# Sixteen overlapped steps per head pair in the stick-breaking layer of a two-layer trunk

## What is computed

```python
logits = einsum('bhqd,bhsd->bhqs', qb, k) * scale        # strict: key before query
log_beta = log_sigmoid(logits)
log_keep = where(strict, log_beta - logits, 0.0)
between = cumsum(log_keep, reverse=True) - log_keep
weights = where(strict, exp(log_beta + between), 0.0)
y = weights @ v
```

## Time and profile before

| | |
|---|---|
| median of 3 runs | 1549.23 us (1548.76 to 1550.56) |
| the profiled execution | 1549.6 us, span 1547.8 us |
| granted TensorE clock, mean | 0.962 |
| prologue, up to the first score | 0 to about 95 us |
| stick layer's eight pairs | about 95 to 770 us |
| output projection, differential layer, its output projection | to 1547.8 us |

### The profile page before, as it was taken

The page is one execution under the profiler, slowest core; times in us unless marked ns, Lnnn a source line. Parts: engine busy times, 40 slices in busy tenths (PEclk is TensorE's granted clock), DMA queues, the critical chain, the costliest instruction groups (busy, mean ns, idle before and its releaser), DMA issues. The chain is left out here.

```text
span 1547.8 us, 23695 instructions
## 1 busy us (share of the span) xinstructions
PE 1394.5 (90%) x7206; PEld 1142.0 (74%) x7206; DVE 1049.6 (68%) x1812; ACT 875.4 (57%) x1710; POOL 558.8 (36%) x334
## 2 busy tenths in 40 slices
PE   6888989898999999986996899999999999995898
PEld 3577777777777777775875678887878878783776
DVE  4559888887969797978558656556565655557415
ACT  4536465555656464555345457667676767667322
POOL 2025546555656465636222412131121212122204
PEclk8889999999999999997998899999999999996999
DMA  9011121112021211121034011000100010002015
GB/s 347 25 54 56 42 62 46 54 50 58 27 74 35 68 41 54 57 98 63 1 123 136 28 38 31 27 27 27 41 27 27 27 41 27 27 14 109 1 52 180
DMA packets 112649, 89.82 MB, mean 58 GB/s; under 512 B 2553, under 2 KB 101090, under 8 KB 112610
## 3 DMA queue, kind: packets, MB, share of 16 engines
q1 hardware_dynamic: 112320, 89.15, 18.3%
q10 hardware_dynamic: 290, 0.18, 0.1%
HBM read 80.92 MB, written 8.40 MB: 58 GB/s over the span
## 5 line engine op out<-in xcount | busy, mean ns | idle before, releaser
L711 PE MATMUL bank<-h_hi,w_hi 128*128 128x512 f32 x976 | 396.8, 407 | 10.9 <-DVE h_lo L612 4.7
L711 PE MATMUL bank<-h_lo,w_hi 128*128 128x512 f32 x976 | 394.2, 404 | 0.0
L711 PE MATMUL bank<-h_hi,w_lo 128*128 128x512 f32 x976 | 391.4, 401 | 0.0
L681 POOL TENSOR_TENSOR w_lo<-w_raw,w_hi 128x1024 fp32r<-128x1024 f32 x59 | 159.7, 2707 | 381.2 <-ACT w_hi L675 381.2
L1323 POOL TENSOR_TENSOR a<-a,stick 128x128 f32<-128x128 f32 (+7 forms) x128 | 188.4, 1476 | 243.3 <-DVE stick L1188 243.3
L1188 DVE TENSOR_TENSOR_SCAN stick<-b 128x128 f32<-128x128 f32 (+7 forms) x128 | 204.9, 1601 | 43.0 <-ACT b L1095 42.9
L711 PEld LDWEIGHTS bank<-h_hi,w_hi 128*128 128x128 f32 x976 | 186.5, 191 | 43.5 <-issue 11.7
L711 PEld LDWEIGHTS bank<-h_hi,w_lo 128*128 128x128 f32 x976 | 186.0, 191 | 33.2
L711 PEld LDWEIGHTS bank<-h_lo,w_hi 128*128 128x128 f32 x976 | 185.9, 190 | 30.5
L1094 ACT ACTIVATE a<-bank 128x512 f32<-128x512 f32 (+2 forms) x192 | 94.7, 493 | 107.8 <-PE bank L998 52.6
L1014 PE MATMUL bank<-ident,a 128*128 128x128 f32 x576 | 89.7, 284 | 44.5 <-POOL a L1323 30.4
(11 more groups left out here) (218 smaller groups left out, 3040.5 us busy)
## 6 DMA issues: line engine op xcount, KB each, us to landing
w_raw<-in_w_in_dram SPq DMA_DIRECT2D x63, 512.0 KB, 4.0
ada_piece<-in_w_ada_dram SPq DMA_DIRECT2D x32, 512.0 KB, 3.8
p_ada<-in_w_ada_dram SPq DMA_DIRECT2D x8, 1024.0 KB, 13.0
wo_raw<-in_w_out_dram SPq DMA_DIRECT2D x8, 1024.0 KB, 8.7
p_x<-in_x_dram SPq DMA_DIRECT2D x8, 512.0 KB, 7.7
o_x<-in_x_dram SPq DMA_DIRECT2D x8, 512.0 KB, 4.2
x_between<-o_res SPq DMA_DIRECT2D x8, 512.0 KB, 2.9
o_x<-x_between SPq DMA_DIRECT2D x8, 512.0 KB, 4.2
```

The costliest lines, as they stand in the source:

```text
L681: self.nc.gpsimd.tensor_tensor(self.m["w_lo"][s][:, :, :], self.m["w_raw"][s][:, :, :], self.m["w_hi"][s][:, :, :].bitcast(F32), ALU.subtr ...
L711: mm = nc.tensor.matmul(self.bank[half][:, :], w[:, k, :], h[:, k, half * HALF:(half + 1) * HALF], start=(i == 0), stop=(i == GROUP - 1))
```

## The change

The pairs overlap. A pair has 16 steps; its last two tiles and two last groups of values are done in steps 0 to 2 of the next pair (`tiles`, `groups`). The projection products, z of the pair, then q, k, v of the next, are spread over all 16 steps so that each step has the same estimated TensorE time. By the new formulas the shares are 12, 16, 5, 14, 12, 14, 7, 14, 12, 16, 9, 14, 12, 14, 7, 14 products. The weights' splits are in step 1 (q), 6 (k), 10 (v) and 13 (the next z). Halves of a kind end in steps 1, 4 (z), 5, 8 (q), 9, 11 (k), 13, 15 (v). Head 0's eight tiles go first, then head 1's, with widths in the order 1, 2, 7, 8, 3, 4, 5, 6 times 128. The values are turned in step 2. VectorE scans before it makes low parts of weights. ScalarE copies q, k, v out of PSUM; a fourth buffer of a, three buffers in which the scan works in place; head 0's q and k are laid out in steps 12 to 14, head 1's in steps 1 to 3 of the next pair, and each head's first score waits for its own alone. The sum of the two halves stays in PSUM, and the gate product reads it there. adaLN comes as eight slices of 128 rows by 512 columns a pair, which VectorE multiplies and adds up; GpSimd has no part in it. GpSimd's split is cut into four instructions. Pair 0 is written out apart (no tiles before it), the last pair keeps 19 steps and another order of its groups.

In the prologue of the loop, ScalarE copies q, k, v of pair 0 too and makes all six layout copies before z's weights. The core of the diff:

```diff
-    m["stick"] = [sb(f"stick{r}", [P, S + 1], F32, 180 + 4.0625 * r) for r in range(2)]
+    m["sa"] = [sb(f"sa{r}", [P, S], F32, 160 + 4 * r) for r in range(4)]
+    m["keep"] = [sb(f"keep{r}", [P, S + 1], F32, 176 + 4.03125 * r) for r in range(3)]
...
-        self.nc.gpsimd.tensor_tensor(self.m["w_lo"][s][:, :, :], self.m["w_raw"][s][:, :, :],
-                                     self.m["w_hi"][s][:, :, :].bitcast(F32), ALU.subtract).then_inc(self.lo_done, 1)
+        for k in range(0, KT, 2):
+            ks = slice(k, k + 2)
+            ins = self.nc.gpsimd.tensor_tensor(self.m["w_lo"][s][:, ks, :], self.m["w_raw"][s][:, ks, :],
+                                               self.m["w_hi"][s][:, ks, :].bitcast(F32), ALU.subtract)
+        ins.then_inc(self.lo_done, 1)
...
+    def hi(self, act, n):
+        h, part = divmod(n, 3)
+        own, other = self.rows(h)
+        src = self.m["uk" if part else "uq"]
+        dst = self.m["k_hi" if part else "q"][h]
+        self.nc.scalar.activation(dst[other if part == 2 else own, :], src[own, :], ACT.Copy).then_inc(self.hi_done, 1)
+    def lo(self, dve, pair, n):
+        h, part = divmod(n, 2)
+        own, other = self.rows(h)
+        m, v = self.m, self.nc.vector
+        dve.wait_ge(self.hi_done, done(6 * pair + 3 * h + part))
+        if part == 0:
+            v.tensor_tensor(m["q"][h][other, :], m["uq"][own, :], m["q"][h][own, :].bitcast(F32),
+                            ALU.subtract).then_inc(self.lo_done, 1)
+        else:
+            v.tensor_tensor(m["k_lo"][h][own, :], m["uk"][own, :], m["k_hi"][h][own, :].bitcast(F32),
+                            ALU.subtract).then_inc(self.key_lo_done, 1)
+            dve.wait_ge(self.key_lo_done, done(2 * pair + h))
+            v.tensor_copy(m["k_lo"][h][other, :], m["k_lo"][h][own, :].bitcast(F32)).then_inc(self.lo_done, 1)
+    def ready(self, pe, pair, h):
+        pe.wait_ge(self.hi_done, done(6 * pair + 3 * h + 2))
+        pe.wait_ge(self.lo_done, done(4 * pair + 2 * h + 1))
...
-    ORDER = [(t // 2 % 2, t // 4 * 2 + t % 2) for t in range(TILES)]
-    CH = [len(widths(i)) for _, i in ORDER]
-    CAT = [sum(CH[:t]) for t in range(TILES)]
-    NCH = sum(CH)
+    LOOP = Order([(h, gg) for h in range(2) for gg in (0, 3, 1, 2)])
+    LAST = Order([(0, 0), (0, 1), (1, 0), (1, 1), (0, 2), (1, 2), (0, 3), (1, 3)])
...
+    KEEP = [t % 3 for t in range(TILES - 1)] + [1]
...
-    EARLY = 3
-    Z = shares(2 * GROUP, [1] * EARLY + [0] * (STEPS - EARLY))
-    QK = shares(4 * GROUP, [0] * EARLY + [7 + ORDER[t][1] for t in range(EARLY, TILES)] + [0] * (STEPS - TILES))
-    V = shares(2 * GROUP, [0] * TILES + [1] * (STEPS - TILES))
-    Z_AT, U_AT, SPLIT_AT = schedule(Z, QK, V, (2, 2, 2))
+    def tiles(p, s, first):
+        t = s - LAG
+        if t < 0:
+            return [] if first else [(p - 1, t + TILES)]
+        return [(p, t)] if t < TILES else []
+    def groups(p, s, first):
+        g, odd = divmod(s - LAG - 2, 2)
+        if odd or (first and g < 0):
+            return []
+        return [(p, g)] if g >= 0 else [(p - 1, g + GROUPS)]
+    def attention(s):
+        i, n = LOOP.tiles[s][1], (s - LAG) % TILES
+        ns = 114 * (i + 1) + 60 + 109 * (LOOP.tiles[n][1] + 1)
+        if s == LAG:
+            ns += 8 * 109
+        if (s - LAG) % 2 == 0:
+            ns += 236 * (2 * LOOP.groups[(s - LAG - 2) // 2 % GROUPS][1] + 2)
+        return ns
+    MATMUL = 227
+    COST = [attention(s) for s in range(TILES)]
+    STEP = (sum(COST) + 8 * GROUP * MATMUL) / TILES
+    WORK = shares(8 * GROUP, [max(0.0, STEP - c) for c in COST])
+    END = [next(s for s in range(TILES) if WORK[s][1] >= (g + 1) * GROUP) for g in range(8)]
+    Z_AT = [[half for half in range(2) if END[half] == s] for s in range(TILES)] + [[]] * (STEPS - TILES)
+    U_AT = [[divmod(g, 2) for g in range(6) if END[2 + g] == s] for s in range(TILES)]
+    SPLITS = [1, END[1] + 2, END[3] + 2, min(END[5] + 2, TILES - 1)]
+    SPLIT_AT = [[kind for kind in range(4) if SPLITS[kind] == s] for s in range(TILES)]
+    LAST_Z = shares(2 * GROUP, [1] * 3 + [0] * (STEPS - 3))
+    LAST_Z_AT = [[half for half in range(2) if LAST_Z[s][0] < (half + 1) * GROUP <= LAST_Z[s][1]] for s in range(STEPS)]
+    HI_AT = {1: (3,), 2: (4,), 3: (5,), TILES - 4: (0,), TILES - 3: (1,), TILES - 2: (2,)}
+    LO_AT = {2: (2,), 3: (3,), TILES - 3: (0,), TILES - 2: (1,)}
+    ADA_AT = {s: k for k, s in enumerate((1, 2, 4, 6, 8, 10, 11, 13))}
+    ADA_GROUP = 5
...
-            def ada(p, i):
-                layer, at = (1, (3 * p + i) * P) if i < 3 else (0, 2 * D + p * P)
-                sp.wait_ge(ada_summed, done(ADA * p + i - 1))
-                sp.dma_start(m["ada_piece"][:, :, :], w_ada[layer, :, bass.ds(at, P)]
-                             .rearrange("(k p) f -> p k f", p=P)).then_inc(ada_in, 16)
-            with sp.Fori(0, PAIRS - 1) as p:
+            def ada(p, *ks):
+                layer, at = (0, 2 * D + (HALF if p else 0)) if isinstance(p, int) else (1, (p - 1) * HALF)
+                for k in ks:
+                    sp.wait_ge(ada_summed, done(KT * p + k - 1))
+                    sp.dma_start(m["ada_slice"][:, :], w_ada[layer, k * P:(k + 1) * P, bass.ds(at, HALF)]
+                                 ).then_inc(ada_in, 16)
+            def pair(p):
                 proj.load(sp, p + 1, 0)
-                ada(p, 0)
+                ada(p, 0, 1, 2)
                 proj.load(sp, p + 1, 1)
-                ada(p, 1)
-                ada(p, 2)
+                ada(p, 3, 4)
                 proj.load(sp, p + 1, 2)
-                ada(p, 3)
+                ada(p, 5, 6, 7)
                 proj.load(sp, p + 1, 3)
-            for i in range(2):
-                ada(PAIRS - 1, i)
+            pair(0)
+            with sp.Fori(1, PAIRS - 1) as p:
+                pair(p)
+            ada(PAIRS - 1, 0, 1, 2, 3, 4)
...
             def values(p, g):
-                h, gg = g % 2, g // 2
-                pe.wait_ge(lo_done, done(NB * p + 2 + CAT[2 * g + 1] + CH[2 * g + 1] - 1))
-                pe.wait_ge(summed, done(GROUPS * p + g - 1))
-                if g % 2:
-                    i = g // 2
-                    pe.wait_ge(ada_summed, done(ADA * p + i))
-                    pe.wait_ge(ada_kept, done(ADA * p + i - 1))
-                    nc.tensor.matmul(O[:, GW:GW + 1], m["ada_sum"][:, :], m["ones"][:, 0:1], start=True,
-                                     stop=True).then_inc(ada_done, 1)
+                h, gg = of(p).groups[g]
+                pe.wait_ge(lo_done, done(last_batch(p, 2 * g + 1)))
+                pe.wait_ge(y_done, done(GROUPS * p + g - 1))
+                if g == ADA_GROUP:
+                    pe.wait_ge(ada_summed, done(KT * p + KT - 1))
+                    for j in range(HALF // P):
+                        mm = nc.tensor.matmul(O[:, GW + j:GW + j + 1], m["ada_acc"][:, j * P:(j + 1) * P],
+                                              m["ones"][:, 0:1], start=True, stop=True)
+                    mm.then_inc(ada_done, 1)
...
+            def share(p, s, project, part):
+                if not project:
+                    f, l = LAST_Z[s]
+                    cut = (f, f + (l - f) // 2, l)
+                    proj.multiply(pe, p, 6 * GROUP + cut[part], 6 * GROUP + cut[part + 1])
+                    f, l = MULTIPLY[s]
+                    cut = (f, (f + l) // 2, l)
+                    outp.multiply(pe, cut[part], cut[part + 1], proj)
+                    return
+                f, l = WORK[s]
+                cut = (f, f + (l - f) // 2, l)
+                f, l = cut[part], cut[part + 1]
+                z = 2 * GROUP
+                proj.multiply(pe, p, 6 * GROUP + min(f, z), 6 * GROUP + min(l, z))
+                proj.multiply(pe, p + 1, max(f, z) - z, max(l, z) - z)
+            def pair(p, first, project):
+                for s in range(TILES if project else STEPS):
                     if s < TILES:
                         score(p, s)
-                    project_share(p, s, project, 0)
-                    if not project:
-                        outp.multiply(pe, MULTIPLY[s][0], sum(MULTIPLY[s]) // 2, proj)
-                    if s >= 4 and s % 2 == 0:
-                        values(p, s // 2 - 2)
-                    if LAG <= s < TILES + LAG:
-                        turn(p, s - LAG)
-                    project_share(p, s, project, 1)
-                    if not project:
-                        outp.multiply(pe, sum(MULTIPLY[s]) // 2, MULTIPLY[s][1], proj)
+                    if s != LAG:
+                        share(p, s, project, 0)
+                    for q, g in groups(p, s, first):
+                        values(q, g)
+                    if s == LAG:
+                        turn_values(p)
+                        share(p, s, project, 0)
+                        share(p, s, project, 1)
+                    for q, t in tiles(p, s, first):
+                        turn(q, t)
+                    if s != LAG:
```

(93 more changed lines are left out.)

196 lines of the change are left out of this document (64 added, 132 removed).

## The result

The changed kernel takes **1650.0 us** (median of 4 runs, 1647.9 to 1651.2) against 1549.5 for the kernel before beside it: a ratio of 1.0647, 95% interval 1.0628 to 1.0665. The forecast was 1583, range 1530 to 1608: the direction was right, the size was not. The profiled execution took 1647.9 us; its span is 98.3 longer than before's.

What follows compares the result with a forecast made beforehand. TensorE bounds the kernel. A middle pair: 73.7 us of work plus 12.5 of stalls, 86.2 instead of 81.4, six times +28.8; pair 0 -3, last pair +8: +34 on 1549.2, so 1583 us, range 1530 to 1608.

Steps and rivals of the forecast that it cites:

- Steps 2, 4, 8, 11 and the seam: Places in a middle pair where TensorE is held: 1.6, 2.0, 2.0, 5.0 and (steps 14 to 16) 1.0 us.
- step 11: v's last product waits for GpSimd's weight split, which may take turns with VectorE: 5.0 us, bounds 2.2 to 5.8.
- step 5's 0.9: In a middle pair, the k subtraction and cast stand ahead of tile 6's low weights: 0.9 us, bounds 0 to 1.0.
- the six places: Stalls of TensorE in steps 2, 4, 5, 8, 11 and 14 to 16: 12.5 us a pair, stated bounds 4.6 and 14.5.
- TensorE's floor stays 73.7: TensorE's own work in a middle pair, summed from single instruction prices, is 73.7 us, unchanged by the edit.
- The clock: Rival: step 11's wait lowers TensorE's granted clock, 2.3 us more in each of seven pairs, 1599 us; chance 0.17.
- The row of the first z product: Kernel before: clock 0.59 over 16 products following a stretch of 5.2 us with 0.8 of work; 6.1 instead of 3.7 us.
- Pair 0: First score sooner, first z product some 0.9 us later, 8.5 us of stalls; pair 1 begins 3 us earlier, bounds -6 and -1.
- Last pair: It inherits 3.5 us of tiles and groups, and output weights leave some 10 us later: +8 us, bounds +4 and +12.
- Edits costed at nothing: Gate product reading PSUM, adaLN sums as eight slices, evictions on ScalarE: all hidden, no cost over a pair.
- waits-fit rival: VectorE's and GpSimd's queues run ahead, split pieces take no turns; lower bounds hold, 78.3 us a pair, 1529 us; chance 0.22.

Runs made afterwards that it cites:

- the better kernel: Changed kernel with both splits earlier, sum's other half copied before values, output weights sooner, head 1's q remainder sooner, adaLN sums moved and loads regrouped: 1532.1 us.
- the filled kernel: Changed kernel plus products nobody reads in the two long waits, 9 before k's first product and 24 before v's: 1620.5 us.
- the last two kernels of the main line: the better kernel, 1532.1 us; then it with head 0's copies and remainders a step sooner, head 1's k remainder later except in the last pair: 1518.7 us.

## Why the prediction was right and where it failed

The profiled execution is 65 us over the forecast: 7 up to pair 1 (-3 forecast, +3.9 measured), 8.3 in each of six middle pairs (+4.8 forecast, +13.1), 8 in the last pair (+8, +16.0). Of the 8.3, the waits are 1.2, TensorE's own work 1.9 and the clock 5.1, a term that the sum put at nothing.

- **Which waits:** right. Steps 2, 4, 8, 11 and the seam have them, the longest before one product in step 11, both long ones ended by GpSimd's low weights.
- **Their sizes:** 2.02, 2.24, 2.58, 5.86 and 1.3 for the seam with step 0, against 1.6, 2.0, 2.0, 5.0 and 1.0; step 5's 0.9 stayed hidden behind step 4's and appeared (0.8) when that fell. Sum 14.0 against 12.5. The picture of step 11, "two column sums and the scan of 1024 (3.6 together) may take turns with the pieces", failed: what was held was the weighing ahead of them (4.53 us for 1.77), so that the nearness of 5.86 to the upper bound of 5.8 is luck. The upper bounds of the six places add up to 15.1, not to the 14.5 stated.
- **"TensorE's floor stays 73.7":** it is 75.6, so 1.9 us went missing in every pair, 11 us in all. The sum of prices leaves out the adaLN products with the column of ones (two of them are why 315.45 to 316.60 in the earlier trace rows is 1.15 us and not 1.01), 0.7 us in a pair of before; most of the rest is in the projection products, 47.8 us from start to start there against 44.2 + 2.5. The trace of before had the better figure: 6.0 us of recorded waits in a pair of 81.4, not 7.5, which leaves 75.4.
- **The clock:** the step that failed most. It was nothing in the sum and stood as a rival with 0.17 and 2.3 us a pair for the wait of step 11 alone; it costs 5.8 in the pair shown (4.1 to 5.9 over six), and three waits have a slow stretch beside them. The sign that the prediction named for this case, a clock under 0.95 in the middle pairs, came (0.91 to 0.945), but its figure, 1599, is short too. The argument "1 us waits left the clock at 1.00" was true of the pair it was read from and said nothing of waits of 2 to 6 us, which the forecast itself had put into every pair. The row of the first z product was the nearer one. This and the floor are 7.7 of the 9.2 us by which the middle pair shown was missed.
- **Pair 0:** the first score came 2.5 us sooner, and the first z product, at 98.44, 1.0 later, as said, with a wait of 5.40 us for its weights (1.81 before). Behind it the first runs of k and v products waited 8.0 us together; all waits there come to 9.7 us against the 8.5 put in. So the sign was not lost by the waits alone: the rest is the floor and the clock, 0.93 here, which no run tells apart. TensorE's waits in pair 0, 92.8 to 184.9 ("issue": the profile shows no releaser):

```profile
PE bank L716 <- issue: 8.0, 2, 5.6
PE bank L716 <- POOL w_lo L685: 5.4, 1, 5.4
```

- **Last pair:** late output weights were right, and worth 7.3 us (894.7 to 887.4 when they alone are moved). The wait of 7.58 us at head 1's first score was not seen: the last pair keeps another order, which needs head 1 in step 4, and this was not held against the layout's new place.
- **Edits costed at nothing:** right in the better kernel, where neither the copies' engine nor the column sums shortened to 8 columns, nor the cut, moves the time by over 3.5 us. In the changed kernel the cut costs 15 us, and a column sum is one of the two instructions beside the weighing that was held. The gate product takes 0.42 us each time, and column sums take over 0.74, both as said:

```profile
L1353 DVE SCALAR_TENSOR_TENSOR ada_acc<-ada_slice,cond_act,ada_acc 128x512 f32<-128x512 f32 x7 | 8.2, 1178 | 0.5 <-DMA ada_slice<-in_w_ada_dram 0.5
...
L1336 DVE TENSOR_TENSOR y<-bank,y 64x256 f32 x8 | 3.4, 422 | 0.9 <-DVE bank L1333 0.2
```

The waits-fit rival was wrong for this kernel. That 1532 and 1519, measured with the splits moved and more, lie beside its 1529 shows only that such times are within the scheme's reach.

What isn't settled: when a wait of some 2 us lowers the clock. In the filled kernel the pair from 272.3 has waits of 2.02 and 2.23 us in steps 2 and 4 and keeps its full clock, and the pair from 453.0 has the same waits at the same places and loses it for 3.4 us behind the second. So neither the length of the wait nor the order of work around it decides alone. And the 0.5 us between the floors of the last two kernels of the main line (78.3 - 2.7 and 76.4 - 1.3) has no cause shown.

## What to carry to other kernels

When a schedule packs the bound engine to the brim, compare the distance between the issue of a helper's work and its first use step by step: here two splits one step too late cost 60 us, where the whole scheme, with this and the other waits put right, gains 18 to 31. Price a repeated wait of some microseconds on TensorE with its slow clock behind it (here 14 us of waits a pair brought 4.1 to 5.9 more), and take the floor as period minus recorded waits, which the trace of the kernel before already gives, not from single prices. After every such move check the special first and last iterations against the new order.

## What the runs showed of the hardware

- TensorE's granted clock fell to half (0.50, 1.2 of 2.4 GHz) for 3.4 to 6.8 us beside waits of 2.0 to 5.9 us in the middle pairs; in the one shown TensorE is busy for 81.4 of 95.4 us. Unread products in the two longest waits brought the pairs' clock from 0.91 to 0.945 up to 0.98 or 1.00 and the kernel from 1650 to 1620.5 us, with 33 products more a pair.
- Waits of up to 0.94 us left it at 1.00 in the pairs of 78.3 us, and waits of up to 1.38 us in five of the six middle pairs of the kernel before. In the sixth it fell for 3.4 us, at 611.0, beside waits of 0.64 and 0.72 us (0.98 over the pair); that pair took 81.42 us, no more than the others, and had 4.7 us of waits instead of 6.0.
- A GpSimd multiplication of two SBUF operands that began 0.03 us before a column sum on VectorE, with a scan behind it, took 4.53 us for 1.77; VectorE's two took 0.73 and 2.27 there, their undisturbed times. It is so in all seven pairs. In step 2 it was the other way round: the column sum took 2.31, and the weighing that began some 0.02 us before it took its 1.77, in all seven pairs again:

```profile
297.59 1.77 POOL L1437 TENSOR_TENSOR sa<-sa,keep 128x896 f32<-128x896 f32 x1 [8.16 <-DVE keep L1309]
```

```profile
297.60 2.31 DVE L1353 SCALAR_TENSOR_TENSOR ada_acc<-ada_slice,cond_act,ada_acc 128x512 f32<-128x512 f32 x1
```

The Trainium skill, "SBUF — State Buffer", section "Who interferes with whom", has such pairs contend, and the trace agrees; which of the two is held, no run here tells in general.
